# Branch projections behind the sample's scan, and the sample's keys turned on TensorE for two of three head groups

## The reference, cut to what matters

```
h = RMSNorm(x);  u = h @ w_in
# columns of u: z (1024) | x,B,C (2048) | dt (16) | q,k,v of 3 head groups | z_att | q_mem | z_mem | gates (3 x 1024)
A: y_ssd = Mamba-2 scan over x,B,C,dt (16 heads x 64, state 128, chunks of 128), D skip, SiLU(z), RMSNorm
B: y_att = sliding-window attention, 3 groups x 8 heads x 64, (window, dilation) = (128,1), (512,4), (2048,16),
           merged by the groups' softmax denominators, times SiLU(z_att)
C: y_mem = attention of 4 heads x 128 into 256 memory tokens, times SiLU(z_mem)
merged = sigmoid(gate0) * (y_ssd @ w_br_ssd) + sigmoid(gate1) * (y_att @ w_br_att) + sigmoid(gate2) * (y_mem @ w_br_mem)
y = RMSNorm(x + merged @ w_out)
```

## Time and profile before

| | |
|---|---|
| median of 3 runs | 2397.36 us (2384.73 to 2397.72) |
| the profiled execution | 2396.68 us, span 2394.9 us |
| busy: TensorE, VectorE, ScalarE, GpSimd | 2154.2, 1066.4, 721.0, 240.9 us |
| mean granted clock of TensorE | 0.93 |
| DMA | 247.59 MB, mean 103 GB/s |

### The profile page before, as it was taken

The page is one execution under the profiler, slowest core; times in us unless marked ns, Lnnn a source line. Parts: engine busy times, 40 slices in busy tenths (PEclk is TensorE's granted clock), DMA queues, the critical chain, the costliest instruction groups (busy, mean ns, idle before and its releaser), DMA issues.

```text
span 2394.9 us, 35765 instructions
## 1 busy us (share of the span) xinstructions
PE 2154.2 (90%) x14762; PEld 1996.3 (83%) x14762; DVE 1066.4 (45%) x2153; ACT 721.0 (30%) x1490; POOL 240.9 (10%) x364
## 2 busy tenths in 40 slices
PE   4899998999699999999988999898999876988997
PEld 4699998989699899999986778338998866987997
DVE  5214665535353534343354882103554554444423
ACT  4223443123423323236441112103343421123202
POOL 1001111000001101112120000001111110000000
PEclk8899999999899999999997989798999977788998
DMA  6211331211011111122353554463333444435422
GB/s 198 73 51 41 104 91 55 77 45 32 28 53 41 58 55 51 62 80 82 133 184 106 178 165 144 135 225 117 98 107 111 139 121 118 142 120 179 152 83 99
DMA packets 166899, 247.59 MB, mean 103 GB/s; under 512 B 19702, under 2 KB 114614, under 8 KB 166710
## 3 DMA queue, kind: packets, MB, share of 16 engines
q1 hardware_dynamic: 144288, 178.91, 24.1%
q0 software_dynamic: 22448, 66.39, 8.5%
HBM read 179.14 MB, written 66.11 MB: 102 GB/s over the span
## 4 chain that ended last, share of the span: by engine, by line
PE 74%; DVE 9%; DMA 6%; issue 5%; ACT 5%; SPq 1%; POOL 0%; DVEq 0%; ACTq 0%; POOLq 0%
PE bank L2102 19%; PE bank L2103 18%; PE bank L2104 18%; PE bank L2269 2%; PE bank L2376 2%; PE bank L2244 2%; PE bank L2227 2%; DVE w_lo L1568 2%; PE bank L2491 1%; ACT w_hi L1273 1%; PE bank L2205 1%; DVE Lm L1993 1%; ACT soft L1398 1%; DMA w_raw<-in_w_in 1%; PE bank L2312 1%
## 5 line engine op out<-in xcount | busy, mean ns | idle before, releaser
L2102 PE MATMUL bank<-w_hi,hT_hi 128*128 128x256 f32 (+1 forms) x2016 | 587.0, 291 | 26.7 <-ACT hT_hi L1381 18.5
L2103 PE MATMUL bank<-w_lo,hT_hi 128*128 128x256 f32 (+1 forms) x2016 | 574.6, 285 | 0.0
L2104 PE MATMUL bank<-w_hi,hT_lo 128*128 128x256 f32 (+1 forms) x2016 | 571.2, 283 | 0.0
L2102 PE MATMUL bank<-hT_hi,w_hi 128*128 128x352 f32 x1344 | 462.1, 344 | 23.5 <-DVE acc L1939 9.7
L2103 PE MATMUL bank<-hT_lo,w_hi 128*128 128x352 f32 x1344 | 446.0, 332 | 0.0
L2104 PE MATMUL bank<-hT_hi,w_lo 128*128 128x352 f32 x1344 | 445.4, 331 | 0.0
L2102 PEld LDWEIGHTS bank<-w_hi,hT_hi 128*128 128x128 f32 (+1 forms) x2016 | 371.3, 184 | 30.2 <-issue 24.0
L2104 PEld LDWEIGHTS bank<-w_hi,hT_lo 128*128 128x128 f32 (+1 forms) x2016 | 371.9, 184 | 1.9
L2103 PEld LDWEIGHTS bank<-w_lo,hT_hi 128*128 128x128 f32 (+1 forms) x2016 | 371.3, 184 | 1.7
L2102 PEld LDWEIGHTS bank<-hT_hi,w_hi 128*128 128x128 f32 x1344 | 265.7, 198 | 38.4 <-issue 12.0
L2103 PEld LDWEIGHTS bank<-hT_lo,w_hi 128*128 128x128 f32 x1344 | 266.4, 198 | 0.5
(11 more groups left out here) (393 smaller groups left out, 3004.9 us busy)
## 6 DMA issues: line engine op xcount, KB each, us to landing
w_raw<-in_w_in SPq DMA_DIRECT2D x96, 512.0 KB, 5.0
kvring<-in_cache_win_kv SPq DMA_DIRECT2D x144, 256.0 KB, 3.4
feat_T<-fstage POOLq DMA_DIRECT2D x40, 528.0 KB, 4.0
fstage<-feat_T SPq DMA_DIRECT2D x16, 528.0 KB, 4.9
kvring<-in_cache_mem_kv SPq DMA_DIRECT2D x32, 256.0 KB, 3.8
xc<-feat_T SPq DMA_DIRECT2D x8, 1024.0 KB, 5.8
o_rows<-obuf POOLq DMA_DIRECT2D x48, 132.0 KB, 2.0
mo<-o_rows SPq DMA_DIRECT2D x24, 264.0 KB, 3.7
```

The lines of the kernel that those rows point to most:

```text
L2102: pe.matmul(out, xh(k), wh(k), start=(k == 0), stop=False)
L2103: pe.matmul(out, xh(k), wl(k), start=False, stop=False)
L2104: ins = pe.matmul(out, xl(k), wh(k), start=False, stop=(k == nk - 1))
```

## The change

**The sample's keys.** Groups 0 and 1 are turned on TensorE like the memory sets: 56 turns (8 + 32 + 16), banks 5 and 6 in turn, evicted by ScalarE for all attention sets. Group 2 keeps its 32 products on VectorE; hi and lo of the query now lie on 64 partitions of one tile `qS`, so that one matmul copies a token's query. Sets of groups 1 and 2 alternate. Scores of groups 0 and 1 land in bank 7, memory's in bank 4; ScalarE copies them all in ssoft.

**The fill.** N_SAMPLE_FILL is 8 instead of 9. Each key set counts 1 in the grouping (four to a place), value sets go five to a place instead of 16. Seven gate chunks are left for the scan and lie over its first 48 entries (up to ssd_sb 0). The other 12 entries have no dense work; ya stands in entries 48 to 51, with loads of its own (`yal`, three slots) from entry 44 on. All of p1 comes behind the scan, with one yb in eight of its eleven stretches.

**Queues and buffers.** xc of the next chunk is loaded at q3, z at q4, the first two sequences' states at chunk 7's q3 and at (8, 0), the later ones at the ssd_sb two before. w_lo of a chunk split in the scan moves behind the next q3. p1's first gates are loaded behind the last yal, p2's first gates and sums when two yb slots are free and accT 0 is stored. acc0 serves tiles 0, 2 and 4, acc1 the others.

```diff
-N_MEM_FILL, N_TAIL_FILL, N_SAMPLE_FILL = 8, 2, 9
+N_MEM_FILL, N_TAIL_FILL, N_SAMPLE_FILL = 8, 2, 8
@@ plan
         sets.append(("att", b, 0, None))
-        for g in (1, 2):
-            sets += [("att", b, g, t) for t in range(TS)]
+        for t in range(TS):
+            sets += [("att", b, g, t) for g in (1, 2)]
...
-        weight += 1 if x[3] is not None else (TS if x[0] == "att" else 2)
+        weight += 1
...
-    side += [sval[i:i + 16] for i in range(0, len(sval), 16)]
+    side += [sval[i:i + 5] for i in range(0, len(sval), 5)]
...
-    core += [[("ssd", NB, q)] for q in (4, 5, 6)] + [[("yb", 2 * k), ("yb", 2 * k + 1)] for k in range(4)]
-    n_gate, n_ya = 31, 4
+    core += [[("ssd", NB, q)] for q in (4, 5, 6)]
+    n_gate, n_ya = 48, 4
+    core[n_gate - 4] += [("yal", k) for k in range(3)]
+    for i in range(n_ya):
+        core[n_gate + i] += [("yal", k) for k in (3 + i, 7) if k < KT8 and (k < 7 or i == n_ya - 1)]
+        core[n_gate + i] += [("ya", 2 * i), ("ya", 2 * i + 1)]
     sched += spread(core[:n_gate], gate_steps(len(fill_src)))
-    for i in range(n_ya):
-        sched += core[n_gate + i] + [("ya", 2 * i), ("ya", 2 * i + 1)]
+    for x in core[n_gate:]:
+        sched += x
...
-    sched += spread(core[n_gate + n_ya:], steps)
+    sched += spread([[]] * 2 + [[("yb", k)] for k in range(KT8)] + [[]], steps)
...
-        later = [k for k in range(i + 1, min(i + 16, len(sched))) if sched[k][0] == "pv"]
+        later = [k for k in range(i + 1, min(i + 16, len(sched))) if sched[k][0] == "pv" or sched[k][0] == "ssd" and sched[k][2] == 3]
@@ ScalarE, VectorE and TensorE: keys
+                elif s[0] == "skey" and s[1] in turn_no and on_act[turn_no[s[1]]]:
+                    v = turn_no[s[1]]
+                    act.wait_ge(s_skt, v + 1)
+                    if v >= 2:
+                        act.wait_ge(s_sks, v - 1)
+                    act.activation(kset[:, v % 2, :, :], bank[5 + v % 2][:, :].rearrange("p (i n) -> p i n", i=4), ACT.Copy).then_inc(s_skA, 1)
...
-                        pe.matmul(bank[3 + x % 4][:, :], one, qSh[:, g, :], start=True, stop=False)
-                        pe.matmul(bank[3 + x % 4][:, :], one, qSl[:, g, :], start=False, stop=True).then_inc(s_qb, 1)
+                    pe.matmul(bank[3 + x % 2][:, :], unit_r[:, tok:tok + 1].broadcast_to([2 * NS, P]), qS[:, :],
+                              start=True, stop=True).then_inc(s_qb, 1)
...
+                        for i in range(4):
+                            if kind == "att":
+                                n0, n1 = (TS * b, TS * b + TS) if t is None else (TS * b + t, TS * b + t + 1)
+                                out = bank[7][:, 256 * g:256 * g + 256].rearrange("p (n h) -> p n h", h=HEADS)[:, n0:n1, 2 * i:2 * i + 2]
+                                ins = pe.matmul(out, kset[:, w % 2, i, :], qbd[:, g, i, n0:n1, :], start=True, stop=True)
@@ SyncE
+                    if k >= 3:
+                        sp.wait_ge(s_yal, k - 2)
+                    sp.dma_start(ya_slot(k), yT[8 + k]).then_inc(s_kv[k % 3], 16)
+                    if k == 7:
                         gates_stored(sp)
+                        for i in range(2):
+                            sp.dma_start(gate1[:, i, :], featT[FT_GATE + 8 * (i + 1)]).then_inc(s_g1, 16)
...
-                elif s[0] == "ssd" and s[2] == 0:
-                    c = s[1]
+                elif s == ("ssd", 0, 0) or s[0] == "ssd" and s[2] == 3 and s[1] < NB:
+                    c = s[1] + 1 if s[2] else 0
...
+                elif s[0] == "ssd_sb" and s[1] + 2 < BS:
+                    sp.wait_ge(s_en, s[1] + 1)
+                    load_prev(s[1] + 2)
```

More of the change, by code:

```diff
@@ L837, in build_program, with keys_evicted @@
         n_att = sum(x[0] == "att" for x in sets)
[L838 to L844, removed]
+        key_prod, turn_no, turn_set = {}, {}, []
+        for n, (kind, b, g, t) in enumerate(sets):
+            if g < 2 or kind == "mem":
+                turn_no[n] = len(turn_set)
+                turn_set.append(n)
+            else:
+                key_prod[n] = (len(key_prod), g, TS * b + t)
+        n_prods, n_turns = len(key_prod), len(turn_set)
+        on_act = [sets[n][0] == "att" or (n - n_att) % 2 == 0 for n in turn_set]
+        def keys_evicted(eng, v):
+            if on_act[v]:
+                eng.wait_ge(s_skA, sum(on_act[:v + 1]))
+            else:
+                eng.wait_ge(s_skD, v + 1 - sum(on_act[:v + 1]))
         dt_cols = fraw_a[0:SH, 3:3 + TOK]
@@ L885, in build_program @@
             gate_no["p2", ft] = n_sig
+        yb_at = (0, 1, 2, 0, 1, 2, 0, 0)
+        acc_use = [sum((f in (0, 2, 4)) == (ft in (0, 2, 4)) for f in range(ft)) for ft in range(KT8)]
+        n_acc = (3, 5)
         def yb_slot(k):
-            return (yraw2, gate2, acc2)[k % 3][:, :]
+            return (yraw2, gate2, acc2)[yb_at[k]][:, :]
         def yst_of(c):
@@ L1035, in _ @@
                             sp.wait_ge(s_yst[i], 16 * (5 - i))
-                    if k >= 3:
-                        sp.wait_ge(s_yal, KT8 + k - 2)
-                    sp.dma_start(yb_slot(k), yT[k]).then_inc(s_kv[k % 3], 16)
+                    if yb_at[k] in yb_at[:k]:
+                        old = max(x for x in range(k) if yb_at[x] == yb_at[k])
+                        sp.wait_ge(s_yal, KT8 + old + 1)
+                    sp.dma_start(yb_slot(k), yT[k]).then_inc(s_kv[yb_at[k]], 16)
                 elif s[0] == "p1" and s[3] == 0 and s[4] == 0:
@@ L1475, in _ @@
                     k = s[1]
-                    act.wait_ge(s_kv[k % 3], kv_loads(k % 3) + 32 + 16 * (k // 3 + 1))
+                    at = yb_at[k]
+                    act.wait_ge(s_kv[at], kv_loads(at) + 16 * len(range(at, KT8, 3)) + 16 * yb_at[:k + 1].count(at))
                     if k == 6:
-                        act.wait_ge(s_p1st[0], 16 * KT8 // 2)
+                        act.wait_ge(s_p1st[0], 16 * n_acc[0])
                     act.activation(yBh[:, k, :], yb_slot(k), ACT.Copy).then_inc(s_yah, 1)
@@ L1569, in split_lo @@
                                   ALU.subtract).then_inc(s_wlo, 1)
-            where = [(g, tok) for n in range(n_att) for _, g, tok in key_prods[n]]
+            where = [(g, tok) for _, g, tok in key_prod.values()]
             def sum_heads(x):
@@ L1934, in _ @@
                     if br == 0:
-                        if ft >= 2 and j == 0:
-                            dve.wait_ge(s_p1st[ft % 2], 16 * (ft // 2))
+                        if acc_use[ft] and j == 0:
+                            dve.wait_ge(s_p1st[ft not in (0, 2, 4)], 16 * acc_use[ft])
                         elif j == 0:
@@ L2325, in _ @@
                         for i in range(4):
-                            ins = pe.transpose(bank[5 + m % 2][:, P * i:P * i + P], kvring[:, n % NRING, P * i:P * i + P], ident)
+                            ins = pe.transpose(bank[5 + v % 2][:, P * i:P * i + P], kvring[:, n % NRING, P * i:P * i + P], ident)
                         ins.then_inc(s_skt, 1)
-                    if m >= 1:
-                        m -= 1
-                        kind, b, g, t = sets[n_att + m]
-                        pe.wait_ge(s_skA if m % 2 == 0 else s_skD, m // 2 + 1)
-                        for i in range(MH):
-                            out = bank[7][:, P * g:P * g + P].rearrange("p (b t h) -> p b t h", t=TS, h=MH)[:, b, :, i]
-                            ins = pe.matmul(out, kset[:, m % 2, i, :], mq[:, i, TS * b:TS * b + TS], start=True, stop=True)
+                    if v >= 1:
+                        w = v - 1
+                        kind, b, g, t = sets[turn_set[w]]
+                        keys_evicted(pe, w)
+                        if turn_set[w] == n_att:
+                            pe.wait_ge(s_km, n_prods)
+                        for i in range(4):
[3 more added lines that the diff above has]
+                                ins = pe.matmul(out, kset[:, w % 2, i, :], qbd[:, g, i, n0:n1, :], start=True, stop=True)
+                            else:
+                                out = bank[4][:, P * g:P * g + P].rearrange("p (b t h) -> p b t h", t=TS, h=MH)[:, b, :, i]
+                                ins = pe.matmul(out, kset[:, w % 2, i, :], mq[:, i, TS * b:TS * b + TS], start=True, stop=True)
```

167 lines of the change are left out of this document (80 added, 87 removed).

## The result

The changed kernel takes 2409.78 us (median of 6 runs, 2403.78 to 2413.92) against 2395.03 for the one before (6 runs, 2383.60 to 2397.72): ratio 1.0083, 95% interval 1.0053 to 1.0113. That is within 1% of no change, but a small loss where I had forecast a gain (2367). The profiled execution took 2405.78, its span is 2403.9.

What follows compares the result with a forecast made beforehand. TensorE's own work, plus its idle and half-clock losses, was taken as the bound. Terms -7.6 (merges, sprep), -51 (keys), +24 (values) and +5 (scan, p1) sum to -29.6: span 2365.3, so 2367 us, range 2340 to 2410.

Steps and rivals of the forecast that it cites:

- 56x1.3 = 72.8: Key stage: 56 turns at 1.3 us, full clock; with broadcasts, dense steps and 8 us for clock falls, 142 us.
- Rival C: Key stage: turned keys hold TensorE at half clock, 2.4 us a turn, +75 us, 2442 us in all; chance 0.05.
- The broadcast's price: Key stage: each of 32 remaining broadcast matmuls takes 0.23 us, bounds 0.23 and 0.47, together 7.4 us.
- SP's wait for s_do: Scan under gates: it stands ahead of the splits' loads but delays nothing; stretch 305.5 us, bounds 290 and 330.
- 42/48x5 = 4.4 feature steps: Scan under gates: dense fill per chunk, 17.1 us plus 15.6 of its own and loss, 32.7 us a chunk.
- Merges and sprep: Stretch before the keys: five z token steps leave it, -7.6 us taken between ends of 0 and -14.6.
- Chunks every 32 to 33 us: Scan under gates: expected sign of the forecast's 32.7 us a chunk; wrong if chunks stay above 36 us.
- ssd_sb every 9 us at clock 0.50: Scan alone: sequences 1 to 7 without dense work at 9.1 us each, 64 of the stage's 85 us.
- rival A: Scan alone keeps the full clock: 62 us instead of 85, 2344 us in all; chance 0.15.
- p1 at 130.5: Branch projections alone: 48 steps, 94 us dense, plus gate waits and slow starts once a tile, 130.5 us.
- rival B: p1 alone never warms up: all 48 steps slow, 178.5 us instead of 130.5, 2415 us in all; chance 0.12.
- Rival D: Scan chunks bound by VectorE's chain: 36 us each instead of 32.7, +26 us, 2393 us in all; chance 0.11.

Runs made afterwards that it cites:

- queue: Changed kernel with the zt load moved to its chunk's own q1 and the last gate chunk's split behind ssd_sb 2: 2398.23 us, ratio 1.0046 to the kernel before.
- place_alone: Kernel before with only the placement changed (scan, p1, eight sample chunks), keys still on VectorE: 2410.41 us, ratio 1.0090 to the kernel before.
- keys_alone: Kernel before with only the sample keys' change and value groups of five, old scan and p1: 2398.29 us, ratio 1.0047 to the kernel before.
- low_back: Changed kernel with the gate weights' low halves straight behind the split, as before the change: 2422.86 us, ratio 1.0141 to the kernel before.
- gates: Changed kernel with the two halves of gate1 loaded apart, each with its own semaphore: 2392.96 us, ratio 1.0018 to the kernel before.

## Why the prediction was wrong

**The step that failed** is the keys' "56x1.3 = 72.8 ... plus 8 for short falls of the clock where a split leaves two key groups side by side". The unit was right (1.31 at full clock), the stage's dense work too (57.4), and the loss was 40 (37 at half clock, 3 idle) instead of 8, outside the bounds 0 to 25 that I gave. I had looked for two groups side by side at splits alone, of which the stage has two, and not at the places that get no step: five runs of two or three groups were the result, 30 of the 40 us. And I had judged by the earlier trace rows, 44.4 us at clock 1.00; but that stretch held more dense work than turns (23.6 against 20.8 us), and the new stage has 57 us of it beside 87 of turns and broadcasts. Rival C named this mechanism, with 83 us (75 and the 8) and a chance of 0.05; half of it happened. The broadcast's price (0.43 against 0.23) is another 6.4 us: the end of my bounds that I did not take.

**The second**, smaller, is the scan's "SP's wait for s_do now stands ahead of the splits' loads, but TensorE posts it in that very step, so nothing waits behind it". I looked at whether the wait for s_do was short and did not follow the other one, zt's for s_dyd, to the weight load behind it, nor asked who stands behind ScalarE's split. The waits of 5.2 and 7.3 us, with the half clock behind the first, are 13.6 us (queue); by the terms of my sum the first lies under the gates and the second in the scan alone. And of the chunk itself, "42/48x5 = 4.4 feature steps" assumed that places and splits don't care where they meet; the steady chunk was 33.3 instead of 32.7.

**Point by point.** Merges and sprep shrank by 17.6 (102.2 to 84.6), not 7.6: more even than the end of -14.6 that I had for it. Chunks every 32 to 33 us: 33.3 at first. ssd_sb every 9 us at clock 0.50: yes, from ssd_sb 2 on the clock is 0.50 and they start 9.0 to 10.9 us apart, so rival A is out. (Its 62 us don't come out of the rows either: seven sequences at 4.9 instead of 9.1 leave 58.) p1 at 130.5: 134.7, with a wait a tile, ended by VectorE's acc product; rival B is out, since its steps ran at 0.88 on average. "No wait on xc": 1.1 us once. Rival D's 36 us per chunk did not come. The key stage "over 165 us" was my sign of being wrong, and it is 184.7. That 2409.78 lies within my range of 2340 to 2410 is luck: the range was wide for rivals A and D, and neither came.

The placement's bill shows in place_alone, and I had not added it up this way: a sequence costs 9.0 us alone and a pair of p1 steps 3.9 more, while in the old order the two side by side took 10.2 (keys_alone, 2078.55 to 2088.77): 4.75 for the sequence at clock 1.00 and 5.47 for the pair at 0.69. That is 2.7 us for each of seven sequences, 19 us, given away by parting them.

The Trainium skill (TensorE: Matmul & The Clock Gate, "Loop structure matters more than you think") lets matmuls run cold when a long DMA wait stands before each. Weighed against p1, the trace again only half agrees: clock 0.88 over the stage, with a wait in seven of its eight tiles. The stage where most of the clock was lost, the keys, had 3.3 us of waits in 184.7.

## What to carry to other kernels

Work taken from VectorE and given to TensorE as transposes and tiny products has to be priced partly at half clock unless dense steps that are needed anyway stand between every one or two of them: in this kernel that took the stage's loss from 40 to 18 us and 9 us off the whole, while extra dense work regained 13 us for 18. Before a load is moved in a queue, list what is issued behind it and who stands behind that on the engine that uses it: the new waits of 5.2 and 7.3 us and the 16 us of low_back each come from a late weight load, and so does about half of the waiting left in gates' p1 (yb and weight loads). And latency-bound work that runs at half clock alone is where fill is cheapest: a pair of dense steps beside each ssd_sb added 1.2 us to its 9.0, a third of the 3.9 that the pair costs alone.

## What the runs showed of the hardware

- TensorE's granted clock falls while the engine is hardly ever idle: 181.39 of 184.7 us busy at 0.79 (the fall at 1294.77 has no gap before it), and 0.65 with eight sets in a row (177.62 of 180.0 busy). Being busy with transposes and the small products did not hold it. In four of the five long runs the dense step behind (352 columns) was back at full clock before its end, 0.16 us a matmul; the one of 256 columns at 1303.48 was at 0.51 throughout. Behind five of the ten groups of four it was the dense step that ran slow (0.65 to 0.74).
- One matmul of 512 columns with 64 rows of stationary copies costs 0.43 us from start to start at full clock, 0.72 at half (1297.84 to 1298.56), where a dense one of 352 columns is 0.163; by columns alone 0.24 would be expected (an estimate from that 0.163).
- Two dense matmuls of 352 columns more beside each turn, 0.33 us to the turn's 1.31, raised the clock of the stage from 0.79 to 0.87.
